# A diagonal state-space recurrence taken four tokens at a time, its rotation back moved from GpSimd to VectorE

## The chip, the cores and the metric

One core of a Trainium2 chip runs the whole program. The metric is the device time of one execution in microseconds (us), taken as the median of three runs. Engines are named as in the profile: PE is TensorE's matmul and PEld its weight load, DVE is VectorE, ACT ScalarE, POOL GpSimd and SP SyncE.

## The reference

Two residual blocks work on `x` of 256 tokens by 2048 features in fp32. Each projects, runs several branches, gates and merges them, and ends in an MLP of width 8192. Nearly all arithmetic lies in the projections. The change touches one branch of the second block, the S5 mixer, and the preparation of its constants:

```python
def s5_mixer(xin, lam_re, lam_im, log_dt, b_re, b_im, c_re, c_im, d, w_glu, b_glu):
    u = xin.reshape(bsz, seq, 64, 16)              # 64 groups of 16 channels
    dt = exp(log_dt)[:, None]; mag = exp(lam_re * dt)
    ab = mag * (cos(lam_im * dt) + 1j * sin(lam_im * dt))    # transition of each state
    k = (ab - 1) / (lam_re + 1j * lam_im)
    bb = k[..., None] * (b_re + 1j * b_im)         # 64 complex states for each group
    bu = einsum('blgh,gph->blgp', u, bb)
    # s[t] = ab * s[t-1] + bu[t], for 256 tokens
    y = einsum('blgp,ghp->blgh', s_re, c_re) - einsum('blgp,ghp->blgh', s_im, c_im)
    g = gelu(y + d * xin)
    return g * sigmoid(g @ w_glu + b_glu)
```

The 64 x 64 = 4096 complex states are 32 tiles of 128 partitions.

## The kernel before

**The stream.** Every weight matrix comes in units of 256 rows by 512 columns (512 KB). SyncE's queue loads a unit into `raw` (4 slots), ScalarE rounds it to `whi` (fp32r), VectorE makes `wlo = raw - whi`, and TensorE does 12 matmuls on it: 2 row tiles, 2 token tiles, 3 products (hi x hi, hi x lo, lo x hi), each 128 x 128 weights by 512 columns (`unit`, L1729 is the helper `mm`). A unit waits for its `wlo`; a slot of `whi` comes free when TensorE has used it. There are 512 units in a block: 256 before its MLP and 256 in it.

**The order.** Each engine's program is written out by position: after each unit every other piece of work (a generator) goes on to the position that it has `yield`ed. So a piece "at 39" stands on its engine behind unit 39 of the block, and all engines keep the order that results. Positions of block 2 are counted from its first unit.

**S5 before.** The factor ab is split into its size `mag` and a rotation. With tables of cos and sin of the angle for 256 tokens, the input is rotated, a real scan with the factor `mag` runs over the tokens, and the result is rotated back:
- GpSimd computes the tables in `make_tables` (L549 to L554) during the MLP of block 1 and stores them to HBM; SyncE loads one table (256 KB) per tile (`tables`, L384), each waiting for the rotation back of an earlier tile.
- `stage_moves2` and `stage_turn2` (L1386) turn the projected input to channels on partitions, `XI`.
- TensorE's `s5_in` computes bu for two tiles at a time, at position 26 + 5m, m = 0 to 15: 4 matmuls with 32 rows of weights by 256 tokens.
- VectorE's `s5` (L1518 to L1526) rotates and scans a tile, 6 instructions; GpSimd in `block2` (L516 to L519) rotates back, 4 instructions, after waiting for the scan; VectorE's scan of tile j waits for GpSimd's tile j-2.
- TensorE's `s5_out` multiplies four tiles with C, 8 matmuls with 32 columns of weights, at position 39 + 10i; VectorE's `skip` (L1533) adds d times the input.
- GpSimd also scales C by k at the start of block 2 (L503 to L508).

Attention of block 2 (`attn2`) runs at positions 70 + 5h for 8 heads, on TensorE, ScalarE and VectorE. The functions that the change touches follow.

Of the kernel before, what the change touches and what calls it, by code (L numbers as in the profile page):

```python
# [15 lines left out]
F32 = mybir.dt.float32  # L16
# [33 lines left out]
def build(nc, A, out):  # L50
    with ExitStack() as ctx:
# [13 lines left out]
        wlo = sb("wlo", [P, RING, UK * CH], F32R)  # L65
        XH = sb("XH", [P, KD, T], F32R)
# [154 lines left out]
        def yready(b, k):  # L221
# [21 lines left out]
        XI, GS, SG = ft(slot(W, 2, 2)), ft(slot(W, 4, 2)), ft(slot(W, 2, 2))  # L243
# [5 lines left out]
        BT = [slot(Z, 2 + r).rearrange("p (i c) -> p i c", i=8) for r in range(2)]  # L249
        CT = [slot(Z, 8 + r).rearrange("p (i c) -> p i c", i=8) for r in range(2)]  # L250
        GW = slot(G, 3).rearrange("p (g c) -> p g c", g=8)
        CTMP = [slot(W, 11), slot(W, 13)]
# [5 lines left out]
        NTAB, TG = 4, 8  # L258
        TAB = [G[:, 512 * i:512 * i + 512].rearrange("p (r t) -> p r t", r=2) for i in range(NTAB)]
        TNEW = [slot(G, 2 * r, 2).rearrange("p (j t) -> p j t", t=T) for r in range(2)]  # L260
        ROT = [slot(W, 7)[:, 512 * i:512 * i + 512].rearrange("p (r t) -> p r t", r=2) for i in range(2)]
        D2 = slot(W, 6)[:, 512:1024].rearrange("p (r t) -> p r t", r=2)
        STATE = [m.rearrange("p (r t) -> p r t", r=2) for m in (
            slot(W, 8)[:, 0:512], slot(W, 6)[:, 0:512], slot(Z, 5)[:, 512:1024], slot(Z, 11)[:, 512:1024],
            slot(G, 2)[:, 0:512], slot(G, 2)[:, 512:1024])]
        NS = len(STATE)
        STMP = slot(W, 8)[:, 512:1024].rearrange("p (r t) -> p r t", r=2)
        PARQ = 104
        S5Q, S5D, HQ2, HD2, GQ = 26, 5, 70, 5, 110
        S5_TILES = 32  # L270
# [10 lines left out]
        TURN2_DST = {(tag, h): slot(W, at + h) for tag, at in (("s5", 2), ("q", 9), ("k", 11)) for h in range(2)}  # L281
# [35 lines left out]
        def block_move(m, src, dst):  # L317

            tq, fq = m // 4, m % 4
            return (dst[B * fq:B * fq + B].rearrange("p (k t q i) -> p t k q i", t=NT, q=4, i=B)[:, :, :, tq, :],  # L320
                    src[B * tq:B * tq + B].rearrange("p t (k q f) -> p t k q f", q=4, f=B)[:, :, :, fq, :])

# [46 lines left out]
        def _(sp_):  # L369
# [6 lines left out]
            def tables():  # L376

                for j in range(S5_TILES):
                    yield S5Q + S5D * (j // 2) - (0 if j % 2 else 3) if j >= NTAB else 6 + j
                    if j == 0:  # L380
                        sp_.wait_ge(S("tables_saved"), 32 * S5_TILES // TG)
                    if j >= NTAB:
                        sp_.wait_ge(S("s5_state_ready"), j - NTAB + 1)
                    sp_.dma_start(TAB[j % NTAB], A["tables"][j]).then_inc(S(f"table_in{j % NTAB}"), 16)  # L384

# [47 lines left out]
        def _(pool):  # L433
# [46 lines left out]
            def block2():  # L480

                pool.wait_ge(used, mlp_base(1, NF - 1))
                for r in range(2):
                    pool.dma_start(BT[r], A["b_t"][r]).then_inc(S("s5_b_in"), 16)
                for r in range(2):
                    pool.dma_start(CT[r], A["c_t"][r]).then_inc(S("s5_c_in"), 16)
# [7 lines left out]
                def by_state(m):  # L494
                    return m.rearrange("p (j c) -> p j c", c=32)

                cre, cim = (by_state(slot(Z, 8 + r)) for r in range(2))
                t1, t2 = (by_state(m) for m in CTMP)
                kr, ki, nkr = (k.unsqueeze(2).to_broadcast([P, 32, 32]) for k in (D_KR, D_KI, D_NKR))
                pool.wait_ge(S("s5_c_in"), 32)  # L500
                pool.wait_ge(S("s5_factors"), 1)
                pool.wait_ge(used, u0[2, "a"] + 8)
                tt(t1, cre, ki, ALU.mult)  # L503
                chain(tt(t2, cim, ki, ALU.mult))
                tt(cre, cre, kr, ALU.mult)
                chain(tt(cim, cim, nkr, ALU.mult))
                tt(cre, cre, t2, ALU.subtract)
                tt(cim, cim, t1, ALU.subtract).then_inc(S("c_scaled"), 1)  # L508
                for j in range(S5_TILES):

                    tab, r, state = TAB[j % NTAB], ROT[j % 2], STATE[j % NS]
                    c, s = (tab[:, i].unsqueeze(1).to_broadcast([P, 2, T]) for i in range(2))
                    pool.wait_ge(S("s5_r_ready"), j + 1)
                    if j >= NS:
                        pool.wait_ge(S("s5_read"), j - NS + 1)
# [4 lines left out]
                    pool.wait_ge(S("s5_state_ready"), j + 1)  # L520
                    if j in (24, 25, 26):
# [9 lines left out]
            def make_tables():  # L531
# [3 lines left out]
                for g in range(S5_TILES // TG):  # L535
                    c, s = TNEW
                    if g:
                        pool.wait_ge(S("tables_saved"), 32 * g)
# [33 lines left out]
            for bi_, b in enumerate(blocks):  # L572
# [23 lines left out]
                if b != blocks[-1]:  # L596
                    make_tables()
# [1543 lines left out]
```

## Time and profile before

| what | value |
|---|---|
| median of three runs | 2969.25 us (2968.87 to 2969.46) |
| the profiled execution's own time | 2969.18 us |
| its span in the profile | 2967.5 us, so 1.7 us lie around it |
| mean granted TensorE clock | 0.999 |
| matmuls recorded | 13302, of which 12576 are those of the units |
| HBM read, written | 574.35 MB, 12.58 MB |

The profile counts from the start of the span. A matmul's end is modelled: 512 columns are shown as 0.39 us long, though the next starts 0.23 us later. So TensorE's cost is read from start to start, and a wait shorter than 0.16 us leaves no idle time in the profile. An fp32 matmul (not fp32r) stands as two MATMUL records with a weight load each. The second block's work before its MLP lies from about 1440 to 2190 us, the S5 stage of it from about 1480 to 1790 us.

### The profile page before, as it was taken

Reading aid. Unit: us, or ns where it says so; the run is one execution under the profiler, and the core shown is the slowest. Engines: PE = TensorE matmul, PEld = TensorE weight load, DVE = VectorE, ACT = ScalarE, POOL = GpSimd, SP = SyncE. Lnnn points to the kernel's source line nnn. Section 1 sums busy time; section 2 is a strip of 40 time slices with the busy share of each in tenths; the row PEclk is TensorE's granted clock in tenths of the full one; section 3 lists DMA queues with packets and bytes.
Section 4 is the critical chain, followed back from the end, with each engine's and each line's share of the span. In section 5 each row is a group of like instructions: output and inputs, shape, how many; then the busy total and the mean of one; then the engine's idle time right before and its main releaser. Section 6 shows DMA issues by size and latency. Waiting matters only on the chain.

```text
span 2967.5 us, 37386 instructions
## 1 busy us (share of the span) xinstructions
PE 2950.7 (99%) x13302; PEld 2428.2 (82%) x13302; DVE 2013.8 (68%) x2104; ACT 1731.3 (58%) x2454; POOL 494.0 (17%) x422
## 2 busy tenths in 40 slices
PE   9999999999999999999999999999999999999998
PEld 7888888888888888888877778888888888888887
DVE  6767654566667777676789996655566666666666
ACT  6776644547655455555665666544557555555555
POOL 1000110110035233320257660110000000000000
PEclk9999999999999999999999999999999999999999
DMA  8656666756666676666855555666665666666664
GB/s 257 182 160 197 198 201 193 201 184 197 194 194 220 191 224 205 208 221 185 268 186 188 186 177 179 215 208 210 205 203 185 200 195 193 192 192 194 192 191 162
DMA packets 298844, 588.43 MB, mean 198 GB/s; under 512 B 18464, under 2 KB 18480, under 8 KB 298352
## 3 DMA queue, kind: packets, MB, share of 16 engines
q1 hardware_dynamic: 292352, 563.61, 61.3%
q0 software_dynamic: 5952, 22.77, 2.5%
q8 instruction: 66, 1.08, 0.1%
q10 hardware_dynamic: 432, 0.62, 0.1%
q14 instruction: 42, 0.34, 0.0%
HBM read 574.35 MB, written 12.58 MB: 198 GB/s over the span
## 4 chain that ended last, share of the span: by engine, by line
PE 93%; DVE 3%; issue 1%; ACT 1%; DMA 1%; POOL 0%; SPq 0%; DVEq 0%; ACTq 0%; POOLq 0%
PE banks L1729 93%; DVE wlo L1115 1%; DMA raw<-in_w_in 1%; DVE W L1526 0%; ACT whi L610 0%; PE banks L1732 0%; DVE W L1518 0%; DVE banks L1519 0%; DVE banks L1521 0%; ACT L610 0%; ACT G L610 0%; ACT W L610 0%; DVE W L1386 0%; POOL G L516 0%; DVE banks L1520 0%
## 5 line engine op out<-in xcount | busy, mean ns | idle before, releaser
L1115 DVE TENSOR_TENSOR wlo<-raw,whi 128x1024 fp32r<-128x1024 f32 x1047 | 1391.9, 1334 | 863.9 <-ACT whi L610 857.0
L610 ACT ACTIVATE whi<-raw 128x1024 fp32r<-128x1024 f32 (+1 forms) x1049 | 1106.9, 1059 | 1047.5 <-PE banks L1729 937.8
L1729 PE MATMUL banks<-whi,Y 128*128 128x512 f32 x4800 | 1484.4, 389 | 0.3 <-DVE W L1214 0.2
L1729 PEld LDWEIGHTS banks<-whi,Y 128*128 128x128 f32 x4800 | 901.0, 188 | 188.1 <-issue 0.9
L1729 PE MATMUL banks<-wlo,Y 128*128 128x512 f32 x2400 | 933.7, 389 | 0.0
L1729 PE MATMUL banks<-whi,XH 128*128 128x512 f32 x1792 | 706.3, 394 | 7.4 <-DVE wlo L1115 6.9
L1729 PE MATMUL banks<-whi,XL 128*128 128x512 f32 x1792 | 698.1, 390 | 0.0
L1729 PE MATMUL banks<-wlo,XH 128*128 128x512 f32 x1792 | 698.0, 389 | 0.0
L1729 PEld LDWEIGHTS banks<-wlo,Y 128*128 128x128 f32 x2400 | 450.6, 188 | 93.2
L1729 PEld LDWEIGHTS banks<-whi,XH 128*128 128x128 f32 x1792 | 336.5, 188 | 87.0 <-issue 10.6
L1729 PEld LDWEIGHTS banks<-whi,XL 128*128 128x128 f32 x1792 | 336.4, 188 | 71.1
L1729 PEld LDWEIGHTS banks<-wlo,XH 128*128 128x128 f32 x1792 | 336.7, 188 | 67.5
L610 ACT ACTIVATE W<-banks 32x256 f32<-32x256 f32 (+1 forms) x532 | 202.6, 381 | 31.5 <-PE banks L1729 21.9
L1661 DVE SCALAR_TENSOR_TENSOR W<-banks,small,W 128x512 f32<-128x512 f32 x256 | 179.8, 744 | 2.2 <-PE banks L1729 2.1
L589 POOL TENSOR_TENSOR W<-W 128x1024 f32<-128x1024 f32 x20 | 63.4, 3172 | 459.8 <-DVE W L1214 459.8
L610 ACT ACTIVATE W<-W 32x256 f32<-32x256 f32 (+3 forms) x254 | 120.0, 473 | 10.6 <-DVE W L1661 3.6
L610 ACT ACTIVATE Z<-W 32x256 f32<-32x256 f32 x208 | 86.2, 414 | 6.1 <-DVE W L1407 3.0
L517 POOL TENSOR_TENSOR W<-W,G 128x512 f32<-128x512 f32 x32 | 61.9, 1934 | 0.0
L549 POOL TENSOR_TENSOR W<-G,W 128x128 f32<-128x128 f32 (+3 forms) x16 | 15.8, 990 | 227.7 <-PE banks L1729 227.1
L610 ACT ACT_TABLE_LOAD x40 | 51.3, 1283 | 2.4 <-PEq L2127 1.7
L610 ACT ACTIVATE Y<-W 128x1024 fp32r<-128x1024 f32 (+1 forms) x41 | 41.3, 1006 | 11.2 <-DVE W L1601 10.6
L1596 DVE TENSOR_TENSOR W<-W 128x1024 f32<-128x1024 f32 x32 | 39.2, 1225 | 12.0 <-ACT W L610 11.5
(256 smaller groups left out, 1187.9 us busy)
## 6 DMA issues: line engine op xcount, KB each, us to landing
raw<-in_w_in SPq DMA_DIRECT2D x383, 512.0 KB, 4.0
raw<-in_w_mlp_up SPq DMA_DIRECT2D x128, 512.0 KB, 3.9
raw<-in_w_mlp_down SPq DMA_DIRECT2D x128, 512.0 KB, 3.8
raw<-in_w_mlp_in SPq DMA_DIRECT2D x128, 512.0 KB, 3.8
raw<-in_w_mlp_out SPq DMA_DIRECT2D x128, 512.0 KB, 3.7
raw<-in_w_branch SPq DMA_DIRECT2D x80, 512.0 KB, 4.6
raw<-in_w_out SPq DMA_DIRECT2D x64, 512.0 KB, 4.3
tables<-G POOLq DMA_DIRECT2D x8, 1024.0 KB, 8.3
```

Source lines behind the costliest of these rows:

```text
L517: chain(tt(STMP, r, s, ALU.mult))
L549: tt(a_, c0, pc, ALU.mult)
L589: tt(m, m, TMP[added % 2], ALU.add).then_inc(S("tmp_added"), 1)
L610: return nc.scalar.activation(out_, in_, f, **kw)
L1115: tt(wlo[:, i % RING, :], raw[:, i % RING, :], whi[:, i % RING, :].bitcast(F32), ALU.subtract)\
L1596: tt(HB[1], HB[0], HB[0], ALU.mult).then_inc(S("hidden_ready"), 1)
L1661: return stt(x, PA[n % 2][t], r2[:, t:t + 1], x, ALU.mult, ALU.add)
L1729: return nc.tensor.matmul(out_, l, r, start=start, stop=stop, **kw)
```

## The change

Four consecutive tokens are taken as one step of the recurrence, with 64 steps in place of 256.

- **Input.** The projected input is laid out as `U`: for each of the 32 tiles the 32 channels of 4 token phases are stacked to 128 partitions, by 64 steps. `s5_in` multiplies it with weights of 128 rows, which hold B times powers of ab; 8 batches of four tiles, 8 matmuls each of 64 columns, at 24 + 9i.
- **Scan.** VectorE rotates, scans (factor `mag` to the fourth, from a table that is 0 where a tile starts) and now also rotates back (4 instructions), all on a batch of four tiles at once, at 26, 27 and 28 + 9i.
- **Output.** `s5_out`, at 30 + 9i, adds for each tile two parts: C times powers of ab times the state before the step (`RW`, two matmuls of 63 columns), and a direct part inside the four tokens (`RE`, one matmul of 64 columns), which also holds d. ScalarE copies the sum out (`YRAW`), and after batches 3 and 7 turns it back to tokens in 16 copies (`token_move`). `skip` is gone.
- **Preparation.** GpSimd's `s5_prepare` replaces `make_tables` and the scaling of C, in the MLP of block 1: tables for 64 steps, then in 8 rounds the stacked B (8 loads, a wait, 6 instructions, a store), in 8 rounds C times the powers (6 instructions, 2 stores), and a last C part with 16 stores. ScalarE and VectorE wait for it ahead of the MLP's last hidden tile.
- **Direct part.** TensorE's `s5_direct` computes it at the end of block 1's MLP: 64 matmuls with 32 columns of weights by 128 columns. VectorE adds d (14 small instructions, at -5), SyncE stores it and loads it back by batch.
- **Loads.** SyncE loads seven pieces per batch (1.6 MB); from the third batch on it waits for `s5_out` of the batch before last.

```diff
-    for j in range(S5_TILES):
-        c, s = (tab[:, i].unsqueeze(1).to_broadcast([P, 2, T]) for i in range(2))
-        pool.wait_ge(S("s5_r_ready"), j + 1)
-        tt(state, r, c, ALU.mult)
-        chain(tt(STMP, r, s, ALU.mult))
-        tt(state[:, 0], state[:, 0], STMP[:, 1], ALU.subtract)
-        tt(state[:, 1], state[:, 1], STMP[:, 0], ALU.add).then_inc(S("s5_state_ready"), 1)
...
 def s5_in():
-    for m in range(16):
-        yield S5Q + S5D * m
-        for r in range(2):
-            for e in range(2):
-                c = c0 + 32 * e
-                ins = mm(PU[e][:, T * r:T * r + T], BT[r][c:c + 32, i, :], XI[c:c + 32, i, :], tile_position=(c, 0))
+    for i in range(S5_BATCHES):
+        yield S5Q + S5D * i
+        pe.wait_ge(S("stage_moved2"), 1 + i // 4)
+        pe.wait_ge(S(f"table_in{i % 2}"), 16 * TAB_DMAS * (i // 2 + 1))
+        for r in range(2):
+            for e in range(4):
+                c = BATCH * r + TQ * e
+                ins = mm(PU[i % 2][:, c:c + TQ], RB[i % 2][:, 512 * r + P * e:512 * r + P * e + P], U[:, 4 * i + e, :])
...
 def s5_out():
-        for r in range(2):
-            for e in range(4):
-                ins = mm(PT[1][c:c + 32, 0:T], CT[r][:, i, c:c + 32], STATE[(4 * i + e) % NS][:, r, :], tile_position=(0, c))
+        yield S5Q + S5D * i + S5L
+        pe.wait_ge(S("s5_state_ready"), i + 1)
+        for e in range(4):
+            y = PT[1][:, TQ * e:TQ * e + TQ]
+            mm(y, RE[i % 2][:, e, :], U[:, 4 * i + e, :], stop=False)
+            for r in range(2):
+                ins = mm(y[:, 1:TQ], RW[i % 2][:, 512 * r + P * e:512 * r + P * e + P], STATE[i % 2][:, r, TQ * e:TQ * e + TQ - 1])
...
+def s5_direct():
+    yield -7
+    pe.wait_ge(S("prep_dma"), 16 * PREP_DMAS)
+    for i in range(8):
+        for r in range(2):
+            for e in range(4):
+                c, j = B * e, 4 * i + e
+                ins = mm(PU[i // 4][c:c + B, P * (i % 4):P * (i % 4) + P], BST[r][:, j, :], CW[r][:, j], tile_position=(0, c))
...
 def tables():        # SyncE
+    for i in range(S5_BATCHES):
+        yield 8 + 3 * i if i < 2 else S5Q + S5D * (i - 2) + S5L + 5
+        if i >= 2:
+            sp_.wait_ge(S("s5_read"), i - 1)
+        sp_.dma_start(RB[i % 2], A["bst"][i]).then_inc(landed, 16)
+        sp_.dma_start(TAB[i % 2], A["tables"][i]).then_inc(landed, 16)
+        sp_.dma_start(RW[i % 2], A["wst"][i]).then_inc(landed, 16)
+        for k in range(PH):
+            sp_.dma_start(RE[i % 2][B * k:B * k + B, :, B * k:P], ...)
...
 def s5a():           # ScalarE
+    for i in range(S5_BATCHES):
+        at = S5Q + S5D * i + S5L + 2
+        yield at
+        act.wait_ge(S("s5_read"), i + 1)
+        a(YRAW[:, BATCH * (i % 4):BATCH * (i % 4) + BATCH], PT[1][:, 0:BATCH]).then_inc(S("s5_y"), 1)
+        if i % 4 == 3:
+            for m in range(16):
+                if m % 4 == 0:
+                    yield at + 1 + m // 4
+                ins = a(*token_move(m, i // 4))
```

The order on three engines follows, where a term of the prediction rests. On TensorE, before, one `s5_out` between two units (`banks` is PSUM, W and Z hold the states and C; each of these stands twice in the profile):

```order
L1729 MATMUL banks<-whi,XL 128x512
L1729 MATMUL banks<-W,Z 32x256 x2
L1729 MATMUL banks<-Z 32x256 x2
L1729 MATMUL banks<-W,Z 32x256 x2
L1729 MATMUL banks<-Z 32x256 x2
L1729 MATMUL banks<-whi,XH 128x512
```

And with the change, one `s5_in`, and three units later one `s5_out`:

```order
L1883 MATMUL banks<-whi,XL 128x512
L1883 MATMUL banks<-W,Z 128x64 x8
L1883 MATMUL banks<-whi,XH 128x512
...
L1883 MATMUL banks<-W,G 128x64
L1883 MATMUL banks<-W,Z 128x63 x2
L1883 MATMUL banks<-W,G 128x64
L1883 MATMUL banks<-W,Z 128x63 x2
```

Every matmul now has 128 columns of weights and 63 or 64 moving columns, where there were 32 rows or 32 columns of weights and 256 moving columns.

On VectorE, before, one tile of the S5 stage (two of them in five units):

```order
L1518 TENSOR_TENSOR W<-banks,G 128x512
L1519 TENSOR_TENSOR banks<-banks,G 128x512
L1520 TENSOR_TENSOR banks<-banks,W 128x256
L1521 TENSOR_TENSOR banks<-banks,W 128x256
L1525 SCALAR_TENSOR_TENSOR W<-small,banks 128x256
L1526 SCALAR_TENSOR_TENSOR W<-small,banks 128x256
L1115 TENSOR_TENSOR wlo<-raw,whi 128x1024
```

And with the change, one batch (one in nine units; the two SCALAR_TENSOR_TENSOR are the scans):

```order
L1672 TENSOR_TENSOR W<-banks,G 128x512
L1673 TENSOR_TENSOR banks<-banks,G 128x512
L1674 TENSOR_TENSOR banks<-banks,W 128x256
L1675 TENSOR_TENSOR banks<-banks,W 128x256
L1219 TENSOR_TENSOR wlo<-raw,whi 128x1024
L1677 SCALAR_TENSOR_TENSOR W<-G,banks 128x256
L1678 SCALAR_TENSOR_TENSOR W<-G,banks 128x256
L1219 TENSOR_TENSOR wlo<-raw,whi 128x1024
L1684 TENSOR_TENSOR W<-W,G 128x512
L1685 TENSOR_TENSOR G<-W,G 128x512
L1686 TENSOR_TENSOR W<-W,G 128x256
L1687 TENSOR_TENSOR W<-W,G 128x256
```

Ten instructions now serve four tiles and spread over three positions; L1684 to L1687 are the rotation back, once GpSimd's.

On ScalarE, before, around position 97, between attention heads 4 and 5 (`W<-banks 128x384` are the heads' steps):

```order
L610 ACT_TABLE_LOAD
L610 ACTIVATE W<-banks 128x384
L610 ACTIVATE whi<-raw 128x1024 x2
L610 ACTIVATE W<-banks 128x384
L610 ACTIVATE W<-W 128x384
```

And with the change (`W<-W 32x256` are the copies of `token_move`):

```order
L686 ACTIVATE whi<-raw 128x1024
L686 ACTIVATE W<-W 32x256 x4
L686 ACT_TABLE_LOAD
L686 ACTIVATE W<-banks 128x384
L686 ACTIVATE whi<-raw 128x1024
L686 ACTIVATE W<-W 32x256 x4
L686 ACTIVATE whi<-raw 128x1024
L686 ACTIVATE W<-W 32x256 x4
L686 ACTIVATE W<-banks 128x384
L686 ACTIVATE W<-W 128x384
```

The copies now stand ahead of the head's first step (the last `W<-banks 128x384` here), on which TensorE's next step of the head waits, and between the `whi`.

## Rows read from the trace of the kernel before

**Rows 1.** The page's part 1: busy time, share of span, instructions.
```profile
PE 2950.7 (99%) x13302; PEld 2428.2 (82%) x13302; DVE 2013.8 (68%) x2104; ACT 1731.3 (58%) x2454; POOL 494.0 (17%) x422
```
**Rows 2.** The page's part 4: shares of the chain that ended last.
```profile
PE 93%; DVE 3%; issue 1%; ACT 1%; DMA 1%; POOL 0%; SPq 0%; DVEq 0%; ACTq 0%; POOLq 0%
```
**Rows 3.** The chain in order of time: start, us, engine, tile, line, count.
```profile
743.26 666.45 PE banks L1729 x2940
...
1861.16 323.74 PE banks L1729 x1428
```
**Rows 4.** Waits of PE, 1480 to 1800 us: total us, times, longest.
```profile
PE banks L1729 <- DVE wlo L1115: 5.6, 7, 0.9
```
**Rows 5.** Timeline of PE around one such wait: start, us, what.
```profile
1566.83 0.39 PE L1729 MATMUL banks<-whi,XL 128*128 128x512 f32 x1
1568.16 0.50 PE L1729 MATMUL banks<-whi,XH 128*128 128x512 f32 x1 [0.95 <-DVE wlo L1115]
```
**Rows 6.** Busy time by engine in two stretches of the S5 stage.
```profile
1520.00:1640.00 120.00, 117.59 (x565) 90.37 (x564) 118.17 (x132) 67.11 (x102) 94.13 (x60) 1.00 0.59 199
1640.00:1800.00 160.00, 156.83 (x802) 123.64 (x801) 143.73 (x178) 109.60 (x134) 95.76 (x68) 1.00 0.57 181
```
**Rows 7.** Timeline of PE: one `s5_in`, between two units.
```profile
1538.49 0.39 PE L1729 MATMUL banks<-whi,XL 128*128 128x512 f32 x1
1538.81 1.13 PE L1729 MATMUL banks<-W,Z 32*128 32x256 f32 x8
...
1540.21 0.39 PE L1729 MATMUL banks<-wlo,XH 128*128 128x512 f32 x1
```
**Rows 8.** Timeline of PE: one `s5_out`, between two units.
```profile
1547.95 0.39 PE L1729 MATMUL banks<-whi,XL 128*128 128x512 f32 x1
1548.26 0.41 PE L1729 MATMUL banks<-W,Z 128*32 128x256 f32 x2
...
1549.61 0.40 PE L1729 MATMUL banks<-wlo,XH 128*128 128x512 f32 x1
```
**Rows 9.** Timeline of PE: four full fp32 matmuls of 128 columns (gMLP).
```profile
1792.82 0.39 PE L1729 MATMUL banks<-whi,XL 128*128 128x512 f32 x1
1793.05 1.05 PE L1729 MATMUL banks<-Z,G 128*128 128x128 f32 x8
...
1794.17 0.40 PE L1729 MATMUL banks<-wlo,XH 128*128 128x512 f32 x1
```
**Rows 10.** Timeline of PEld: seven loads on end (attention); four for 8 moving columns.
```profile
1659.05 0.19 PEld L1729 LDWEIGHTS banks<-WR,NONE 128*128 128x128 f32 x1
...
1659.72 0.19 PEld L1729 LDWEIGHTS banks<-wlo,XH 128*128 128x128 f32 x1
...
40.18 0.52 PEld L1729 LDWEIGHTS banks<-small,Z 16*128 16x128 f32 x4 [0.35 <-issue]
```
**Rows 11.** Groups of DVE, S5: count, busy us, mean ns, idle before.
```profile
L1518 DVE TENSOR_TENSOR W<-banks,G 128x512 f32<-128x512 f32 x32 | 21.7, 679 | 1.4 <-PE banks L1729 1.4
L1525 DVE TENSOR_TENSOR_SCAN W<-small,banks 128x256 f32<-128x256 f32 x32 | 22.0, 687 | 1.1
L1520 DVE TENSOR_TENSOR banks<-banks,W 128x256 f32<-128x256 f32 x32 | 13.8, 432 | 1.1
```
**Rows 12.** Timeline of DVE in block 1's MLP, without and with GpSimd at work.
```profile
853.25 1.23 DVE L1115 TENSOR_TENSOR wlo<-raw,whi 128x1024 fp32r<-128x1024 f32 x1 [1.49 <-ACT whi L610]
...
904.93 12.88 DVE L1115 TENSOR_TENSOR wlo<-raw,whi 128x1024 fp32r<-128x1024 f32 x5 [0.61 <-ACT whi L610]
```
**Rows 13.** A group of ACT: copies of 32 partitions by 256.
```profile
L610 ACT ACTIVATE Z<-W 32x256 f32<-32x256 f32 x208 | 86.2, 414 | 6.1 <-DVE W L1407 3.0
```
**Rows 14.** A group of POOL, 512 columns.
```profile
L517 POOL TENSOR_TENSOR W<-W,G 128x512 f32<-128x512 f32 x32 | 61.9, 1934 | 0.0
```
**Rows 15.** A DMA issue of POOL: count, KB, median us to landing.
```profile
tables<-G POOLq DMA_DIRECT2D x8, 1024.0 KB, 8.3
```
**Rows 16.** Waits of SP's queue: total us, times, longest.
```profile
SPq L384 <- POOL W L519: 58.6, 10, 9.6
```

More of the change, by code:

```diff
@@ L1505, in s5_params @@
                     chain(tt(dst, D_U, D_D, ALU.mult))
[L1506 to L1517 removed]
+                chain(ts(D_NKR, D_KR, -1.0, None, ALU.mult))
@@ new lines, in s5_params @@
+                yield PARQ + 17
+                p0, p1, p2 = ((PLO[:, 0, k], PLO[:, 1, k]) for k in range(3))
+                nc.vector.memset(POW[:, 0, 0], 1.0)
+                nc.vector.memset(POW[:, 1, 0], 0.0)
+                for r in range(2):
+                    tt(POW[:, r, 1], mag, p0[r], ALU.mult)
+                chain(tt(MAG2, mag, mag, ALU.mult))
+                for r in range(2):
+                    tt(POW[:, r, 2], MAG2, p1[r], ALU.mult)
+                chain(tt(MAG4, MAG2, MAG2, ALU.mult))
@@ L1890, in s5_out, with s5_rows @@
-            def s5_out():
-                for i in range(8):
-                    yield S5Q + 2 * S5D * i + 13
-                    pe.wait_ge(S("s5_state_ready"), 4 * i + 4)
-                    if i == 0:
-                        pe.wait_ge(S("c_scaled"), 1)
-                    else:
+            def s5_rows():
+                yield PARQ + 21
+                pe.wait_ge(S("s5_params_by_dve"), 5)
+                for r in range(2):
+                    ins = tr(PU[0][:, P * r:P * r + P], POW[:, r, 0:4].rearrange("p k j -> p (k j)"))
+                ins.then_inc(S("s5_rows_mm"), 1)
@@ new lines, in s5_direct @@
+            def s5_direct():
+                yield -7
+                pe.wait_ge(S("prep_dma"), 16 * PREP_DMAS)
+                for i in range(8):
+                    for r in range(2):
+                        for e in range(4):
+                            c, j = B * e, 4 * i + e
+                            ins = mm(PU[i // 4][c:c + B, P * (i % 4):P * (i % 4) + P], BST[r][:, j, :],
+                                     CW[r][:, j].rearrange("p k c -> p (k c)"), start=r == 0, stop=r == 1,
+                                     tile_position=(0, c), skip_group_check=True)
+                ins.then_inc(S("e_mm"), 1)
@@ L1897, in s5_out @@
+            def s5_out():
+                for i in range(S5_BATCHES):
+                    yield S5Q + S5D * i + S5L
+                    pe.wait_ge(S("s5_state_ready"), i + 1)
+                    if i:
                         pe.wait_ge(S("s5_y"), i)
@@ L2029, in mlp @@
                 after = blocks[blocks.index(b) + 1:][:1]
-                pairs = [Steps(x_pairs(after[0], "a"))] if after else []
+                pairs = [Steps(s5_direct()), Steps(x_pairs(after[0], "a"))] if after else []
                 if after:
@@ L2063, in _ @@
                 gens = pairs + [Steps(g) for g in ((
-                    [lru(), attn1()] if b == 1 else [s5_in(), s5_out(), attn2(), gmlp(), glu_out()])
+                    [lru(), attn1(), s5_rows()] if b == 1 else [s5_in(), s5_out(), attn2(), gmlp(), glu_out()])
                     + [merge(b, before)])]
```

379 lines of the change are left out of this document (250 added, 129 removed).

## The prediction

> **What bounds the kernel.** I read the page's busy times first, then the chain that ended last, then TensorE's waits, and then the S5 stage. TensorE is busy for 2950.7 of 2967.5 us [rows 1] and has 93% of the chain [rows 2]: the time is the sum of TensorE's matmuls and little else. The long stretches of the chain give the pitch: 666.45 us for 2940 matmuls and 323.74 us for 1428, both 0.227 us each [rows 3], so a unit of 12 is 2.72 us. A change can gain only where TensorE waits or where its own small matmuls get shorter, and it loses by every matmul that it adds.
>
> In the S5 stage there are such waits. TensorE waited there 7 times for `wlo`, 5.6 us as shown [rows 4]. The reason is VectorE: between 1520 and 1640 us it was busy for 118.17 of 120 us, and GpSimd for 94.13 [rows 6]. One wait is shown in full: a matmul starts 1.33 us after the one before it, where 0.23 is the pitch [rows 5]. The profile calls only 0.95 of this idle, as it draws a matmul 0.39 us long; with 0.16 us more for each of the seven, and some short waits that do not show, the stage loses about 7 us. That is what the change can win at most on that side.
>
> **TensorE's own work, which decides.** From the last matmul of a unit to the second of the next, less two pitches of 0.227:
> - `s5_in` before: 1540.21 - 1538.49 - 0.45 = 1.27 us [rows 7], 16 times: 20.3 us.
> - `s5_out` before: 1549.61 - 1547.95 - 0.45 = 1.21 us [rows 8], 8 times: 9.7 us. The matmuls with 32 columns of weights run four side by side: 16 records of 256 columns in 1.2 us.
> - Removed in all: 30.0 us.
>
> The new matmuls have 128 columns of weights and 64 moving ones. No row of before has this shape. Bounds: four fp32 matmuls with 128 moving columns cost 1794.17 - 1792.82 - 0.45 = 0.90 us, or 0.112 for each of 8 records [rows 9]. If a record is as long as its moving columns take, half the columns cost 0.056; if its weight load sets the length, it stays 0.112. The nearest rows speak for the load: where seven loads follow on end, behind matmuls of 128 and 256 columns, they start at even steps, 0.67 us for six, 0.112 each, and the four loads of a matmul with only 8 moving columns [rows 10] take 0.52 us, which is three steps of 0.11 and the last load's own 0.19. I take 0.112.
> - `s5_in` now: 8 matmuls, 16 records, 1.79 us, 8 times: 14.3 us.
> - `s5_out` now: 12 matmuls, 24 records, 2.69 us, 8 times: 21.5 us.
> - `s5_direct`: 128 records with 32 columns of weights, four side by side, 32 rounds. By the rows of `s5_out` a round of 256 columns is 0.22 us and entering costs 0.35 [rows 8]; 128 columns: 32 x 0.11 + 0.35 = 3.9 us, and 7.4 if a round does not shrink.
> - `s5_rows`: two transposes, 0.3 us with the entry, by the same 0.112.
> - Added: 40.0 us. Net **+10 us** on the engine that sets the time, between +9 and +14; with 0.056 a record, the low end, it would be -8.
>
> **VectorE and GpSimd in the stage.** A tile cost VectorE twice each of 0.68, 0.43 and 0.69 us [rows 11], 3.6 us, 32 times: 115 us. A batch costs the same six at the same sizes and four more for the rotation back, for which the nearest rows give 2 x 0.68 + 2 x 0.43 [rows 11]: 5.8 us, 8 times: 46 us. VectorE gets 69 us back in a stretch of some 300 us. GpSimd leaves the stage, and with it a second cost: a `wlo` takes 1.23 us alone, and five in a row took 12.88 us, 2.6 each, while GpSimd worked [rows 12]. So the 7 us of waits should go: **-7 us** (between -8 and -4, as some could hang on the order and not on the load). Spreading a batch over three positions leaves TensorE two units, 5.4 us, for each 2.2 us of S5 and a `wlo` of 1.2, so no batch should make TensorE wait. Nobody else waits for the rotation back but `s5_out`, two positions later.
>
> **What is late next.** ScalarE gains 8 copies out of PSUM and 32 copies of `token_move` at 0.414 us [rows 13], and 16 of those, 6.6 us, stand at positions 96 to 99, ahead of head 5's steps and of `whi`. From 1640 to 1800 us ScalarE was busy for 109.60 of 160 us [rows 6], so of four units with a head's matmuls, some 13 us, about 4 are free. The rest, some 3 us, I take as lost by TensorE; between 0, if ScalarE is far enough ahead, and 5. The first 16 copies stand before the attention and I cost them at nothing: there ScalarE has 1.66 us free in each unit of 2.72, less the staging copies.
>
> At the end of block 1's MLP TensorE does `s5_direct`, and VectorE must then do 14 small instructions between two sums that TensorE needs two units later. VectorE's work there, about 2.6 us by the 0.43 us of 256 columns and less, and one `wlo` and two sums of some 1.4 us, just fills 5.4 us: 0.5 us, up to 2. In that MLP GpSimd's bursts slow VectorE [rows 12]; before, bursts of the same kind cost TensorE nothing, but eight of the new ones start at the middle of a chunk, ahead of sums that TensorE needs two units later: 0.5 us, up to 3. Together the new waits are **+4 us**, from 0 to 9.
>
> **Costed at nothing.** GpSimd's preparation: about 100 instructions of 512 columns at 1.93 us [rows 14], the tables and the last C part, some 270 us, and a dozen round trips of DMA at 8.3 us [rows 15] and their issue, some 150 us. The MLP lasts 666 us [rows 3], and by the positions that it waits for it ends some 70 us before it is needed. If that cover were gone, ScalarE, VectorE and TensorE would all stand. SyncE's six waits for `s5_out` hold up the units queued behind them, with 1.6 MB of tables ahead of the next unit. Before, SyncE stood for GpSimd as long as 9.6 us at a time [rows 16], and all of TensorE's waits in the stage were for VectorE [rows 4]; now I reckon 3 to 4 us of spare. VectorE's small instructions on the powers and the input's other layout replace the like.
>
> **Sum.** 10 - 7 + 4 = +7 us on the profiled execution's 2969.18 us (span 2967.5 and 1.7 around it), which lies 0.07 us under the median of 2969.25: 2976 us, slower by 0.23%. About 0.2%, 6 us, is what a measurement of this kernel can tell from no change, so "same" reaches from 2963.3 to 2975.2 and my time lies just above it.
>
> **Rivals.**
> 1. *ScalarE's copies are covered.* Then the new waits shrink to the 1 us of the boundary and the bursts: 10 - 7 + 1, 2973 us, not slower in a measurement. It decides by how far ScalarE is ahead at position 96: a lead of over 3 us on TensorE's need is enough. For it: ScalarE's idle time around each head. Against it: a head's steps wait for TensorE, so that ScalarE cannot run ahead of them. 0.29.
> 2. *Moving columns set the length, not the weight loads.* At 0.056 us a record `s5_in` is 0.90 and `s5_out` 1.34 us, 17.9 us for all; with 4.2 for the two others 22, so -8 in place of +10, and -8 - 7 + 4 gives 2958 us, faster. For it: rows 9 fit both. Against it: the even steps of rows 10. The Trainium skill, "TensorE: Matmul & The Clock Gate", section "Back-to-back issue gap", gives for an isolated matmul N/2.4 + 2.5 ns, with a floor near 60 cycles up to 64 columns; that would make about 0.058 us of a record of two passes (an estimate by that page) and land where this rival does. The same section says that at small N this leaves out the weight load, and the loads at 0.112 us in this trace agree with that caution. 0.07.
> 3. *The waits stay.* The stage's waits came from the order (a unit's `wlo` behind S5 work that waits for TensorE), or the loads behind SyncE's waits come late, 1 to 2 us in each of six batches. Then nothing is won and the new waits come on top: 10 + 4, up to 10 + 9: 2983 to 2988 us. For it: seven instructions of SyncE and 1.6 MB stand ahead of a unit. Against it: VectorE's load falls by more than half. 0.16.
> 4. *The preparation is not done in time*: all engines stand at the end of the MLP, tens of us. 0.03.
>
> **How the numbers follow.** The forecast has 0.45 and spreads from 2973 to 2981, with two parts in three above 2975.2. Slower: 0.30 of it, and rivals 3 and 4: 0.47 (rounded from 0.49, as some of rival 3 is partly won). Same: the rest of the forecast and nearly all of rival 1: 0.44. Faster: rival 2 and a little of rival 1: 0.09. The range from 2969 to 2988 us leaves out rival 2, the lowest of rival 1 and rival 4. Without rivals 2 to 4 it would be 2970 to 2981.
>
> **What would show it.** TensorE's records: 0.11 us from start to start inside `s5_in` and `s5_out` (0.056 means rival 2). TensorE's waits for `wlo` between 1480 and 1700 us gone; VectorE under 75% busy there; `wlo` at 1.23 us. Waits near position 96 to 104, with ScalarE full. No wait at the end of the MLP over 2 us. I am wrong in kind if TensorE's records in the stage take less time than before, or if its waits grow beyond 10 us.

## The result, and the profile after

The changed kernel takes **3023.03 us** (median of 5, 3022.58 to 3024.84), the kernel before 2969.25 (2968.83 to 2969.46): a ratio of 1.0182 (95% interval 1.0168 to 1.0196), 54 us slower. The prediction was 2976, with 2988 as its upper end. TensorE does what was forecast; 50 of the 54 us are losses for which the prediction had put 4 us, most of them far from the S5 stage.

The page's part 1 and part 4 after (to be held against [rows 1, 2]):

```profile
PE 2977.6 (99%) x13496; PEld 2465.2 (82%) x13496; DVE 1930.9 (64%) x2022; ACT 1760.9 (58%) x2494; POOL 393.4 (13%) x331
...
PE 90%; DMA 4%; DVE 2%; issue 2%; ACT 2%; SPq 0%; DVEq 0%; ACTq 0%
```

The chain now holds 4% of DMA. In order of time it has nine such transfers between 940 and 1160 us, one for each of the 8 rounds of the stacked B and one at the loads of C that follow; before, one piece of TensorE of 666 us stood there [rows 3]. Four of the nine:

```profile
944.77 11.55 DMA raw<-in_w_mlp_down
970.36 9.97 DMA raw<-in_w_mlp_up
994.21 13.04 DMA raw<-in_w_mlp_down
...
1148.46 10.67 DMA raw<-in_w_mlp_down
```

Busy time by engine from 940 to 1180 us, in block 1's MLP, after and then before (PE, PEld, DVE, ACT, POOL, clock, DMA share, GB/s):

```profile
940.00:1180.00 240.00, 215.16 (x900) 173.59 (x900) 163.07 (x125) 113.79 (x160) 149.42 (x137) 0.96 0.78 223
```

```profile
940.00:1180.00 240.00, 240.00 (x1061) 198.72 (x1060) 172.54 (x145) 133.45 (x187) 93.81 (x102) 1.00 0.64 201
```

TensorE starts 161 matmuls fewer in these 240 us; at 0.227 us each **36.5 us** are lost here. This is two thirds of the result. A second count agrees: both traces hold all 12576 matmuls of the units, and held against each other one by one the changed kernel is late by 0.4 us at 940 us, 38.3 at 1190, 46.7 behind the end of the MLP, and 53.5 from 1900 us to its end.

In the S5 stage it went as forecast. The same clock times as [rows 6], after (the changed kernel is 47 us late by then, so the work in them is that of earlier units):

```profile
1520.00:1640.00 120.00, 120.00 (x598) 101.72 (x597) 66.50 (x74) 87.28 (x132) 0.00 (x0) 1.00 0.66 209
1640.00:1800.00 160.00, 159.96 (x825) 136.06 (x823) 86.79 (x109) 109.60 (x146) 1.62 (x3) 1.00 0.59 187
```

VectorE falls from 118.17 to 66.50 of 120 us (68.03 from 1567 to 1687 us, where the work is nearer to that of before), GpSimd is idle, and TensorE's waits for `wlo` [rows 4] are gone from 1480 to 1760 us. The timeline of PE, one `s5_in`, one `s5_out` and the `s5_direct`:

```profile
1549.95 0.39 PE L1883 MATMUL banks<-whi,XL 128*128 128x512 f32 x1
1550.18 1.89 PE L1883 MATMUL banks<-W,Z 128*128 128x64 f32 x16
...
1552.20 0.39 PE L1883 MATMUL banks<-wlo,XH 128*128 128x512 f32 x1
...
1568.11 0.39 PE L1883 MATMUL banks<-whi,XL 128*128 128x512 f32 x1
1568.34 0.33 PE L1883 MATMUL banks<-W,G 128*128 128x64 f32 x2
...
1571.25 0.39 PE L1883 MATMUL banks<-wlo,XH 128*128 128x512 f32 x1
...
1453.43 0.39 PE L1883 MATMUL banks<-whi,Y 128*128 128x512 f32 x1
1453.75 3.70 PE L1883 MATMUL banks<-XF,W 128*32 128x128 f32 x128
1457.72 0.40 PE L1883 MATMUL banks<-wlo,Y 128*128 128x512 f32 x1
```

By the prediction's own way of reading, `s5_in` costs 1552.20 - 1549.95 - 0.45 = 1.80 us (1.79 forecast), `s5_out` 1571.25 - 1568.11 - 0.45 = 2.69 (2.69), `s5_direct` 1457.72 - 1453.43 - 0.45 = 3.84 (3.9).

Two smaller losses stand beside the large one. At the copies of `token_move`, the timeline of ACT and of PE:

```profile
1791.00 2.67 ACT L686 ACTIVATE W<-W 32x256 f32<-32x256 f32 x4
1793.68 1.06 ACT L686 ACTIVATE whi<-raw 128x1024 fp32r<-128x1024 f32 x1
1794.77 2.67 ACT L686 ACTIVATE W<-W 32x256 f32<-32x256 f32 x4
1797.45 0.49 ACT L686 ACTIVATE W<-banks 128x384 f32<-128x384 f32 x1
```

```profile
1799.81 0.39 PE L1883 MATMUL banks<-whi,XL 128*128 128x512 f32 x1
1802.13 0.39 PE L1883 MATMUL banks<-WR,NLOW 128*128 128x256 f32 x1 [1.93 <-DVE WR L1697]
...
1803.74 0.50 PE L1883 MATMUL banks<-whi,XH 128*128 128x512 f32 x1 [0.71 <-DVE wlo L1219]
...
1807.97 0.39 PE L1883 MATMUL banks<-whi,XL 128*128 128x512 f32 x1
1810.48 0.50 PE L1883 MATMUL banks<-whi,XH 128*128 128x512 f32 x1 [2.13 <-DVE wlo L1219]
```

A copy takes 0.67 us here, not 0.414 [rows 13]; the head's step waits behind eight of them, and TensorE for that step and then for two `wlo`. At the end of the MLP VectorE stands for TensorE, and then TensorE for VectorE's sums:

```profile
1457.52 0.73 DVE L1655 COPY W<-identR 32x32 f32<-32x32 f32 x4 [5.81 <-PE banks L1883]
```

```profile
1463.08 1.07 PE L1886 MATMUL banks<-identR,W 128*128 128x128 f32 x4 [2.69 <-DVE W L1815]
```

### The profile page after: what moved, and what is told of

The parts are those of the page before. It is cut to its first block, busy times and chain, and to the rows that moved or that the text cites. A ratio compares the mean times of both kernels' runs of the same rounds, so it can differ in the third digit from the quotient of the medians.

```text
span 3021.1 us, 37563 instructions
## 1 busy us (share of the span) xinstructions
PE 2977.6 (99%) x13496; PEld 2465.2 (82%) x13496; DVE 1930.9 (64%) x2022; ACT 1760.9 (58%) x2494; POOL 393.4 (13%) x331
## 4 chain that ended last, share of the span: by engine, by line
PE 90%; DMA 4%; DVE 2%; issue 2%; ACT 2%; SPq 0%; DVEq 0%; ACTq 0%
PE banks L1883 89%; DMA raw<-in_w_mlp_down 2%; DMA raw<-in_w_mlp_up 1%; DVE wlo L1219 1%; ACT W L686 1%; ACT whi L686 1%; PE banks L1886 0%; DVE W L1815 0%; DMA raw<-in_w_in 0%; DVE W L1750 0%; DVE Y L1760 0%; ACT G L686 0%; ACT L686 0%; SPq L406 0%; SPq L430 0%
## 5 line engine op out<-in xcount | busy, mean ns | idle before, releaser
L1219 DVE TENSOR_TENSOR wlo<-raw,whi 128x1024 fp32r<-128x1024 f32 x1047 | 1358.4, 1302 | 959.5 <-ACT whi L686 953.1
L686 ACT ACTIVATE W<-W 32x256 f32<-32x256 f32 (+3 forms) x286 | 141.1, 494 | 9.6 <-DVE W L1815 3.6
L686 ACT ACTIVATE Z<-W 32x256 f32<-32x256 f32 x176 | 73.0, 415 | 5.6 <-DVE W L1516 3.0
L637 POOL DMA_DIRECT2D W<-in_b_gate x12 | 6.5, 542 | 309.6 <-DVE G L1301 147.9
L1760 DVE TENSOR_TENSOR Y<-W,Y 128x1024 fp32r<-128x1024 f32 x32 | 43.4, 1355 | 2.4 <-ACT Y L686 2.4
```

The lines of the kernel that those rows point to most:

```text
L637: pool.dma_start(bias_buf(n, k), A["b_gate_2"][0, k, CH * n:CH * n + CH].partition_broadcast(P))\
L686: return nc.scalar.activation(out_, in_, f, **kw)
L1219: tt(wlo[:, i % RING, :], raw[:, i % RING, :], whi[:, i % RING, :].bitcast(F32), ALU.subtract)\
L1760: tt(YL[:, kt:kt + 4, :], ft(HB[0]), YH[:, kt:kt + 4, :].bitcast(F32), ALU.subtract)\
```

## How one round makes TensorE wait

The longest wait, read on four engines. GpSimd stores a round's B (512 KB), issues the next eight loads (1 MB) right behind it, waits for them and computes (timeline of POOL):

```profile
992.12 0.60 POOL L546 DMA_DIRECT2D bst<-XF  x1 [0.30 <-POOL XF L596]
...
1007.52 1.26 POOL L591 TENSOR_TENSOR XF<-XF 128x512 f32<-128x512 f32 x1 [10.52 <-DMA XF<-in_b_rows]
...
1018.21 0.60 POOL L546 DMA_DIRECT2D bst<-XF  x1 [0.30 <-POOL XF L596]
```

So this round lasts 26 us (the others 24 to 29), and GpSimd loads or computes in all of it. In these 15 us of transfers the weights come late (timeline of ACT), and when they are there, GpSimd computes and VectorE's `wlo` takes up to 2.3 us (timeline of DVE); the sum that TensorE needs at unit 12 of the chunk stands behind it, and TensorE (timeline of PE) waits 4 us:

```profile
1002.16 1.06 ACT L686 ACTIVATE whi<-raw 128x1024 fp32r<-128x1024 f32 x1 [6.46 <-DMA raw<-in_w_mlp_down]
1007.35 1.06 ACT L686 ACTIVATE whi<-raw 128x1024 fp32r<-128x1024 f32 x1 [4.13 <-DMA raw<-in_w_mlp_down]
```

```profile
1011.06 2.29 DVE L1219 TENSOR_TENSOR wlo<-raw,whi 128x1024 fp32r<-128x1024 f32 x1 [1.20 <-ACT whi L686]
1013.68 1.86 DVE L1219 TENSOR_TENSOR wlo<-raw,whi 128x1024 fp32r<-128x1024 f32 x1 [0.34 <-ACT whi L686]
1015.47 1.40 DVE L1815 SCALAR_TENSOR_TENSOR W<-banks,small,W 128x512 f32<-128x512 f32 x2
```

```profile
1012.55 0.39 PE L1883 MATMUL banks<-whi,Y 128*128 128x512 f32 x1
1017.00 0.79 PE L1883 MATMUL banks<-whi,Y 128*128 128x512 f32 x1 [4.06 <-DVE W L1815]
```

Then TensorE runs at half its clock for a while (windows: the clock is the third number from the end):

```profile
1017.00:1022.50 5.50, 5.50 (x13) 4.34 (x14) 5.50 (x5) 1.88 (x4) 5.20 (x9) 0.50 0.71 213
```

13 matmuls in 5.5 us, where 24 would fit: behind this wait of 4 us, 2.5 us more are lost. Which of the two, loads or arithmetic, is to blame is not in the profile: both stand there in every round. That is what the first runs ask.

## The experiments

All are made from the changed kernel unless it is said otherwise; times are medians, to be held against 3023 and against 2969 for the kernel before.

**Loads left out, arithmetic left out.**

```diff
...
-                    for k in range(PH):
+                    for k in range(PH if g == 0 else 0):      # x1: the loads of rounds 1 to 7
...
+                    if g == 0:                                # x2: the six instructions of rounds 1 to 7
                         tt(BTMP[0], ai, bi_, ALU.mult)
...
```

> Leaves out the eight loads of rounds 1 to 7 of the stacked B (the arithmetic and the stores of these rounds still run, on old data). In the changed kernel TensorE loses 37 us between 950 and 1190 us, 46 us less 3.7 of direct part and what the end of the MLP costs. Theory A (the eight loads of a round, 1 MB, share the DMA engines with the weight stream, raw lands late): the waits before the C part go, some 28 us, and those at 1160 to 1180 us, where two more loads of 512 KB follow, go or stay: 2986 to 2995 us. Theory B (GpSimd's arithmetic slows VectorE's wlo and sums): nothing goes, 3018 to 3025 us.

> Leaves out the arithmetic of rounds 1 to 7 of the stacked B (six GpSimd instructions each); loads and stores stay where they are, so B of these rounds is wrong. Theory A (loads): TensorE still loses over 25 us between 950 and 1190 us, 3012 to 3023 us; rounds may come somewhat closer together. Theory B (GpSimd's arithmetic): the waits go, 2986 to 2995 us.

Measured, one run each: 2990.3 without the loads, 2991.3 without the arithmetic. The first agrees with theory A, the second with theory B: leaving out either takes away 32 to 33 us. TensorE's waits from 740 to 1400 us (engine, line, waited for: us, times, longest), in the changed kernel, without loads, and without arithmetic:

```profile
PE banks L1883 <- DVE W L1815: 20.7, 6, 4.1
PE banks L1883 <- DVE wlo L1219: 4.1, 2, 2.4
```

```profile
PE banks L1883 <- DVE W L1815: 2.3, 1, 2.3
```

```profile
PE banks L1884 <- DVE W L1816: 3.3, 2, 1.8
```

Neither theory stands alone. Busy time from 940 to 1180 us, without loads and without arithmetic (to be held against the two rows of the same stretch above):

```profile
940.00:1180.00 240.00, 237.69 (x1043) 196.38 (x1042) 174.37 (x143) 129.74 (x179) 137.41 (x90) 0.99 0.71 222
```

```profile
940.00:1180.00 240.00, 236.70 (x1035) 194.88 (x1034) 157.97 (x142) 127.99 (x176) 85.02 (x104) 0.99 0.85 250
```

Without the loads GpSimd is still busy for 137.41 of 240 us, and without the arithmetic the DMA engines are busier than in the changed kernel (0.85 and 250 GB/s, not 0.78 and 223); TensorE loses little in either. The arithmetic also stretches a round: without it GpSimd waits for the next position, and the rounds come 22 to 25 us apart with 7 to 12 us of rest in each.

**Loads two at a time, rounds further apart.**

```diff
-                    pool.wait_ge(used, mlp_base(1, 4 + g // 2) + 4 + 8 * (g % 2))
                     for k in range(PH):
+                        pool.wait_ge(used, mlp_base(1, 3) + 4 + 14 * g + 2 * k)
...
-                    pool.wait_ge(used, mlp_base(1, 8 + g // 2) + 4 + 8 * (g % 2))
+                    pool.wait_ge(used, mlp_base(1, 10) + 4 + 6 * g)
...
```

> Same loads, bytes and arithmetic, but the eight loads of a round come two at a time, two units (5.4 us) apart, a round every 14 units in place of about 9, from earlier on; C rounds every 6 units. Theory A (it is the burst): raw keeps up, TensorE loses under 4 us in the MLP before its last units: 2984 to 2990 us. Theory A2 (it is the sum of bytes that is too much for the DMA engines): most of the waits stay, only further apart: over 3000 us. Theory B (arithmetic): the 12 us bursts of GpSimd are the same, so the waits stay: over 3010 us.

Measured: 2989.0 (2987.8 to 2993.3). The waits of the rounds go but for one of 0.9 us; one of 3.4 us stays, where the two loads of C and two rounds of its arithmetic follow without a pause. Theory A's number, but the run changes the burst and the pitch of the rounds at once, and with them where the rounds begin (earlier) and the pitch of the C rounds. The four runs that follow keep the last two changes and part the first two.

**Burst, burst with late arithmetic, lump, and double arithmetic.** All have rounds of 14 units (38 us), which begin as early as in the run before, with C rounds every 6 units.

```diff
+                    pool.wait_ge(used, mlp_base(1, 3) + 4 + 14 * g)       # x8: all eight loads at once
...
+                    pool.wait_ge(used, mlp_base(1, 3) + 4 + 14 * g + 8)   # x9 alone: ahead of the arithmetic
...
+                    if g:                                                 # x12 alone: store ahead of the loads
+                        dma(A["bst"][g - 1], BOUT)
...
+                    for _ in range(2):                                    # x15 alone: the six instructions twice
```

> So far: without the loads (x1) or without the arithmetic (x2) nearly all of the waits in the MLP go, and with the loads two at a time (x3) too. Open: do the two act together because the arithmetic begins as the loads land, while raw is still late (theory C), or did x2 and x3 go well only because a round's loads no longer follow right behind the store and the loads of the round before (theory D)? Here a round has 14 units, as in x3, but its eight loads go out at once and the arithmetic follows them as they land. Theory C: rounds still cost TensorE several waits, at the sums of a chunk: 8 to 35 us between 880 and 1240 us, 2995 to 3020 us. Theory D: under 5 us there, 2984 to 2992 us.

> As the burst run, but the arithmetic of a round waits until 8 units behind its first load (22 us), when raw has caught up. Theory C: the waits go, under 5 us between 880 and 1240 us, 2984 to 2992 us. If the arithmetic or the loads alone were enough to make waits at this place: as the burst run.

> As the burst run (rounds of 14 units, loads at once, arithmetic behind them), but the store of a round (512 KB) is held back until the next round begins, right ahead of its eight loads (1 MB), as it fell out in the changed kernel. Bytes, number of transfers and arithmetic per round are the same. Theory D1 (what counts is the lump of 1.5 MB on end, which the raw stream has to live through with its 7 us of lead): the waits come back, 10 to 30 us in the MLP, 3002 to 3018 us. Theory D2 (what counts is bytes over time, which the longer round has lowered): as the burst run, 2990 to 2998 us.

> Theory E, which the runs so far leave: each round takes lead from the stream twice, first its loads (raw comes late), then its arithmetic (wlo takes about 2.3 us, so that VectorE, with the sums, needs more than the 2.72 us of a unit and can win nothing back), and TensorE waits where the next round begins before the lead is back. In the changed kernel a round has 25 us and GpSimd loads or computes in nearly all of it; without the arithmetic (x2) 11 of 22 us are free, in the burst run some 13 of 38. Here the burst run's arithmetic is done twice (the same values again), so that of 38 us only some 3 are free; bytes and lumps are as in the burst run. Theory E: waits come back, 3003 to 3020 us. If the lumps or the bytes over time set the waits: as the burst run, 2990 to 2999 us.

The last column has TensorE's matmuls between 940 and 1180 us in the trace (1061 before, 900 in the changed kernel); in these runs the stretch holds rounds 2 to 7 and, but for the last run, the loads of round 8.

| run | us, median (lowest to highest) | matmuls |
|---|---|---|
| burst | 2994.8 (2991.2 to 2997.7) | 1061 |
| late arithmetic | 2995.7 (2993.3 to 2999.8) | 1052 |
| lump of 1.5 MB | 2999.4 (2998.0 to 3001.3) | 1033 |
| double arithmetic | 3011.4 (3009.4 to 3013.6) | 1005 |

The burst run lies on the edge of theory C (2995, where theory D ended at 2992 and theory C began at 2995), so its time alone settles nothing. Its trace says more: at the longer pitch these six rounds cost TensorE nothing, and its three waits lie at the first round, the last and C. The late arithmetic settles it against theory C: moved out of the way of the loads it gains nothing. Its expectation had for that case that loads or arithmetic alone make waits here; the two runs without one of them, with a wait or two left, do not bear that out for the changed kernel. The lump comes between its two expectations, 4.6 us above the burst run: it counts little, if at all. The double arithmetic, with the same loads and bytes, brings 17 us back, inside theory E's range. TensorE's waits from 880 to 1240 us, burst and double:

```profile
PE banks L1883 <- DVE W L1815: 5.9, 3, 2.6
```

```profile
PE banks L1884 <- DVE W L1816: 14.3, 8, 3.8
PE banks L1884 <- DVE wlo L1220: 1.3, 2, 0.7
```

So three things together make the loss: a round's loads, its arithmetic, and the next round close behind. Taking away any one of the three was enough for 28 to 34 us. The account that fits: the loads take lead from the weight stream (lead: how long before TensorE's need a unit is ready), the arithmetic lets little be won back, and the next round begins before the lead is there. Lead itself is not in the profile; what speaks for it is that ScalarE stood for weights for 66.8 of the 240 us above in the changed kernel (5.3 before), and from 880 to 1240 us for 24.3 in the burst run and 68.2 in the double one, whose loads are the same.

Not all of it is shown. Held matmul by matmul against before, the double run's loss is uneven: 4.9 us in the first round, at most 1.5 in each of rounds 2 to 6, 7.2 in round 7 and 3.8 in round 8, although GpSimd goes on without a pause behind rounds 3, 4 and 6. So the missing rest is not all, and how much is due to 1.5 MB every 25 us in place of every 38 stays open. Arithmetic doubled without the loads was not run.

**The sums earlier on VectorE.**

```diff
-                    for i in range(7, 14):
+                    for i in range(7, 13):
                         lo(base, i)
                     add(base, 0)
+                    lo(base, 13)
                     lo(base, 14)
                     square(j + 1)
+                    add(base, 1)
                     lo(base, 15)
-                    add(base, 1)
```

> The changed kernel with one other order on VectorE in the MLP: the sum of the first two column blocks of a chunk stands ahead of the wlo of unit 13 (15) and not behind it. TensorE's waits in the MLP are drawn at units 12 of a chunk, which need the first sum, so that the sum has only about 1.5 us to spare where a wlo is 5.6 us ahead. Theory (it is the sum behind a late wlo that TensorE waits for): each such wait is shorter by up to 1.2 us and a part falls under the bound: 8 to 25 of the 37 us go, 2998 to 3015 us. Rival (it is the late raw itself, the sum is only the name in the profile): under 4 us go, 3018 us or more.

Measured: 3019.0 (3016.7 to 3021.7), 4 us less, the rival's time. The waits become more (9 for the sums where there were 6, and 8 for `wlo` where there were 2), but their total stays (26.5 us and 24.8): the sum is where the lateness shows, not where it comes from.

**The copies of `token_move` further apart, gelu behind the heads.**

```diff
-                            if m % 4 == 0:
-                                yield at + 1 + m // 4
+                            n = 4 if i == 3 else 2
+                            if m % n == 0:
+                                yield at + 1 + m // n
...
-                yield at + 5
+                yield at + 18
...
```

> The second set of 16 token copies on ScalarE comes two per position (96 to 103) and not four (96 to 99), and the gelu at 113, behind the last attention head, not at 100 between heads 6 and 7. Theory (ScalarE's order is the price): the 8.6 us that TensorE loses between 1799 and 1815 us, half clock included, go: 3013 to 3016 us. Rival (the heads' own chain is late, whatever stands ahead): under 2 us go, 3021 to 3023 us.

Measured: 3017.1 (3009.0 to 3020.1). The total says little: the four runs lie 11 us apart, and in the profiled one, the fastest, TensorE does 973 matmuls from 940 to 1190 us where the changed kernel does 937, some 8 us, though this edit does not touch that part. By the trace, from the matmul ahead of the last `s5_out` to that ahead of the head's step 12 units later, the changed kernel takes 1830.51 - 1781.30 = 49.21 us and this one 1816.66 - 1771.87 = 44.79: 4.4 of the 8.6 us are gone. Half confirmed. What is left are waits of 1.57, 1.30 and 0.70 us, with two copies still ahead of a `whi` or a head's step; that two a position are still too many is likely, but no run moved them alone.

**All mended.** Loads two at a time and C's loads apart, sums earlier, copies on GpSimd and gelu later, and the small sums of the direct part later (the last two edits are shown):

```diff
...
-                yield -5
+                yield 3
                 dve.wait_ge(S("e_mm"), 1)
...
+                        ins = nc.gpsimd.tensor_copy(*token_move(m, h))
```

> Mended version: loads two at a time and the C loads one by one, the sums earlier, the token copies on GpSimd and gelu behind the heads, the small sums of the direct part behind the MLP's last sums (position 3 in place of -5, with the store at 6 and the first loads at 11). If the loss is made of these three (37 in the MLP, 8.6 at the copies, 4.6 at the MLP's end) and the rest is TensorE's own work: before 2969, plus 6.2 for s5_in and s5_out, plus 3.7 for the direct part, less the 8 us of waits of the stage: 2970 to 2974 us. If a wait stays that these do not explain: over 2978 us.

Measured: **2971.63** (10 runs, 2970.76 to 2973.01), the kernel before beside it 2968.99, ratio 1.0009 (0.9999 to 1.0018); as expected. Its page, part 4:

```profile
PE 99%; ACT 0%; DMA 0%; DVE 0%; issue 0%; SPq 0%; DVEq 0%; ACTq 0%
```

From 740 to 1500 us no wait of TensorE is listed, and the stretch at the copies takes 1779.62 - 1739.15 = 40.47 us, 8.7 less than in the changed kernel. The transfers and bytes are the same. Held matmul by matmul against before, this version loses nothing in the MLP (the changed kernel 37.9 us), 3.9 at its end (8.4), and wins 2.3 from there to the end of the attention. What is left against before, 2.6 us, is what TensorE's own work adds (10) less the waits of the stage that are gone; the interval of the ratio does not rule out nought. No version beat the kernel before.

**Who rotates back.** Once in the mended version, GpSimd again in place of VectorE, and once in the kernel before, VectorE in place of GpSimd:

```diff
+                s5_back(0, 4)                  # x13, GpSimd: the four instructions of batches 0 to 3
...
+                    tt(state, r, c, ALU.mult)  # x14, VectorE, behind the scans of each tile
+                    chain(tt(STMP, r, s, ALU.mult))
```

> The mended version with the rotation back on GpSimd again (four instructions for each of the 8 batches, some 6 us by the old rows), nothing else changed. Theory (with four tokens a step VectorE and GpSimd both have room in the stage, so it does not matter who does it): within 1.5 us of the mended version, 2970 to 2974 us. Rival (GpSimd's work slows wlo again, and s5_out comes late): waits in the stage, 2975 to 2985 us.

> The kernel before with one part of the change alone: the rotation back of its 32 tiles on VectorE, GpSimd idle in the stage. By the rows VectorE then has 32 x (3.6 + 2.2) for the tiles and 81 units at 1.23 us of wlo, 286 us, in a stretch of some 250; before it has 32 x 3.6 and wlo at about 2 us, 277 us. Theory (what GpSimd's work costs wlo is nearly what the rotation costs VectorE): 2970 to 2990 us. Rival (wlo does not get faster without GpSimd): over 3010 us. If the rotation on VectorE is a gain by itself: under 2967 us.

Measured: 2971.89 (2971.16 to 2973.26) for the mended version with GpSimd, the same; 3022.99 (3020.33 to 3023.79) for the old kernel with VectorE, 54 us slower: the rival's number, over 3010, but not its reason, as `wlo` did get faster. The waits of TensorE there from 1480 to 1860 us, and `wlo` from 1520 to 1640 us (ns min, median, max):

```profile
PE banks L1726 <- DVE wlo L1104: 42.9, 20, 3.2
```

```profile
L1104 DVE TENSOR_TENSOR wlo<-raw,whi x33: 1183/1219/1226, 1522.4 to 1639.6; 128x1024 fp32r<-128x1024 f32 x33
```

It takes 1.22 us for a median of 1.71 in the same window before; but with 85 units at about 0.5 that gives back some 40 us and not the 60 that I had counted, against 32 x 2.2 = 70 for the rotations, and VectorE also stood 12 us for TensorE ahead of its tiles: 70 - 40 + 12 = 42, where the listed waits grew by 42.9 - 5.6 = 37. The other 17 us are for the most part half clock: the granted clock is 0.94 from 1520 to 1640 us, 0.96 to 1800 and 0.97 to 1860, where it was 1.00, which by an estimate from these rows is 7 + 6 + 2 = 15 us. So moving the rotation, in this order, is worth nothing by itself: it is the step of four tokens that makes room for it, and then either engine will do.

## Why the prediction was wrong

- **TensorE's work, +10**: right. 0.112 us for a record with 64 moving columns, not 0.056; rival 2 is out. `s5_in`, `s5_out` and `s5_direct` came within 0.1 us each.
- **The waits of the stage, -7**: right. No wait from 1480 to 1760 us; the mended version, in which the three losses below are gone, stands at +2.6 where 10 - 7 gives +3. Rival 3 is out.
- **"Costed at nothing: GpSimd's preparation"**: the step that failed. I asked whether it ends in time, and it did: its last transfers were issued at 1360 us, and nobody waited for them. I did not ask what its transfers take from SyncE's, though their number follows from the change as it is described: 64 loads of 128 KB and 8 stores in a row, 12 MB in 206 us, beside a stream of 192 GB/s (512 KB every 2.72 us). A median weight load between 940 and 1180 us went from 3.7 and 3.9 us (down, up), before,

```profile
raw<-in_w_mlp_down SPq DMA_DIRECT2D x46, 512.0 KB, 3.7
raw<-in_w_mlp_up SPq DMA_DIRECT2D x42, 512.0 KB, 3.9
tables<-G POOLq DMA_DIRECT2D x4, 1024.0 KB, 8.3
```

to 7.4 and 5.4 in the changed kernel:

```profile
raw<-in_w_mlp_down SPq DMA_DIRECT2D x39, 512.0 KB, 7.4
raw<-in_w_mlp_up SPq DMA_DIRECT2D x36, 512.0 KB, 5.4
```

- **"before, bursts of the same kind cost TensorE nothing: 0.5 us, up to 3"**: the second half of the same fault. The bursts before had pauses of up to 33.6 us, no loads among them and only the four stores above; [rows 12] show that they slow VectorE, not that the new ones are like them. The kind was not the same. 37 us in place of 0.5. No rival of mine had this mechanism, and so the range could not hold it.
- **ScalarE's copies, +3 (0 to 5)**: right in place and cause, too small. 3.1 and 2.3 us of waits beyond the pitch and the rest half clock behind them: 8.7 by the mended version. I took the duration of another copy (0.414 for 0.67 us) and no loss of clock.
- **The end of the MLP, +0.5 (up to 2)**: right in place, too small. VectorE came to the small sums before TensorE had done `s5_direct`, so VectorE first stood 5.8 us and had no lead left: 3.2 us of wait and 1.3 of half clock, 4.5, which the mended version does not have.
- **SyncE's waits**: right. Six, up to 7.4 us each (before up to 9.6 [rows 16]), and no wait of TensorE behind them.

The sum by rows: 10 - 7 + 36.5 + 8.7 + 4.5 = 53, of 54 measured. The terms that were right make 3 of it; the three that were too small, or put at nothing, make the rest.

## What to carry to other kernels

Where a stream sets the time, a piece of work that is "hidden" has to be priced by what it takes from the stream: how late each transfer and each slowed instruction makes it, and how long it has to catch up before the next one comes. An end in good time says nothing of that. Read the durations of a moved instruction from rows of the same operands, and look for half clock behind the waits of TensorE.

## What was not expected of the hardware

- GpSimd's transfers lengthen SyncE's: with some 60 GB/s of them beside it (12 MB in 206 us), a weight load of 512 KB took up to 13 us by the chain, where it takes 3.7; without the loads of rounds 1 to 7 the median from 940 to 1180 us is 4.5 and 3.8 us (down, up) in place of 7.4 and 5.4. The Trainium skill, "DMA: Bandwidth & Descriptors", section "Queues, rings and completion order", says that a DMA engine takes turns between the queues that have work for it, a packet at a time. The trace agrees in so far as the queue with less to move held up the one with more; the turns themselves are not shown by a row here.
- VectorE's instructions on two inputs in SBUF stretch while GpSimd computes: `wlo` from 1.23 to 2.3 us, and once the square of the hidden layer, 1.2 us by its median, to 5.9 (a row of VectorE in the changed kernel; ns min, median, max):

```profile
L1750 DVE TENSOR_TENSOR W<-W x15: 1209/1225/5895, 765.6 to 1393.6; 128x1024 f32<-128x1024 f32 x15
```

The Trainium skill, "SBUF — State Buffer", section "SBUF: two separate sides", says that the two engines share a pair of ports which one of them holds for a whole instruction. The longest row agrees: the square stretches by 4.7 us, and beside it GpSimd does four instructions of 1.1 us on end (1170.58 to 1174.75), so the wait would be for several of them and not for one.
- After a wait of 4 us TensorE ran at half clock (0.50, the lower of its two levels) for some 5 us; after one of 2.4 us a few units earlier (at 1009.92) it did not, its next matmuls start 0.23 us apart. The length of a wait does not decide it alone: after the waits of 2.69 us at 1463.08 and 2.13 us at 1810.48 the clock is 0.51 (1463.1 to 1466.4) and 0.50 (1811.3 to 1814.7).
